# State-space entry of a two-block network: the norm's scale and shift applied by channel behind the turns

## The chip, the cores and the metric

One core of a Trainium2 chip. The metric is the device time of one execution in microseconds, the median of three runs where runs are given.

## What is computed

A first block of two layers (a gated delta rule with a feed-forward network; a state-space mixer, "S5", with a mixture of 8 experts) is followed by a second block with its own mixers and 32 experts. Sequence 256, width 1024, all in float32. The change is at the border of the first network and the S5 mixer, which the reference writes as

```
x = layer_norm(ALPHA * x + swiglu(x, w1, w3, w2), ln_g[0, 1], ln_b[0, 1])
u = x @ s5_w_in                      # 1024 x 1024
... per group of 16 channels a complex diagonal recurrence, read out, gelu, GLU ...
x = layer_norm(ALPHA * x + h, ln_g[1, 0], ln_b[1, 0])
```

with `layer_norm(x, g, b) = (x - mean) * rsqrt(var + eps) * g + b`. The normed x is needed twice: turned (channels on partitions) as the operand of `x @ s5_w_in`, and in rows (tokens on partitions) as the residual that the next sum uses.

## The kernel before

The 256 rows lie in `xres` as two halves of 128 tokens on partitions, 1024 channels along the free axis. A quarter is 512 channels of a half. Products keep about float32 accuracy by splitting every operand into a rounded high part and a low remainder: high by high, high by low and low by high are summed in PSUM. ACT copies the high part (`dn_high`), DVE subtracts to get the low one (`dn_low`), in place in the weight ring. The ring holds three units of 128x4096, loaded by SP, each when the unit three before it has been used. The high parts have three buffers taken in turn, so `dn_high` of piece p waits until PE has used piece p - 3.

The order of each engine's work is written out by hand; semaphores link the engines.

**Norm before S5.** `ffn_vector` (L1295) sums and takes statistics half by half (L1319, L325 to L342); ACT takes the root (`norm_root`, L379). DVE's `norm_half` (L348) then computes the rows in two passes a half with the scale row `lnp[:, 0]` (L355) and the shift row `lnp[:, 1]` (L359); both are loaded by SP late in the network (L3390), because their place serves as a weight buffer until then. PE turns each 128x128 block by a transpose (`turn_half`, L386, transposes at L392) into banks 0 to 3. ACT evacuates a quarter at a time into `xT_r`, rounded (`turn_evacuate`, L421), and DVE subtracts that from PSUM to make the low part `s5_x_low` (L1326).

**PE around it** (program order from L3462 on): last products of the network, `own_step` and the router sums (which need nothing of x), `awake(16, 4)`, turn of half 0, `awake(6, 4)`, turn of half 1. `awake(n, b)` issues n products of the identity whose result nobody reads. Each shows as two records.

**`s5_tensor`** (L1532). The input product has eight pieces of 128 output channels. `projected(c)` makes one: 24 matmuls, into bank 0 or 1 in turn; `dn_columns_high` does the 16 that need only the high part of x, `dn_columns_rest` the other eight. ACT evacuates each to `uT`. `driven(q)` multiplies channels into states, 64 small matmuls, into banks 2 to 5, for q = 0 to 7. The order is: piece 0, piece 1, drive 0, piece 2, piece 3, drive 1, piece 4, ... , and `driven(0)` first waits for `ln_scaled` at 6 (L1543), because bank 5 holds the router sums until DVE has read them (`router_sums_vector`, L1496: L1500 and L1501; the second raises `ln_scaled` to 6).

**`s5_vector`** (L1733) begins with `dn_low` of piece 3, `router_sums_vector`, and then rounds: turn the drive by cosines and sines (L1745, L1746), `dn_low` of two more pieces, sum (L1752, L1753), scan (L1761), turn back (L1770, L1771), sum (L1777, L1778).

**`s5_scalar`** (L1646) and **`s5_gpsimd`** (L1720): ACT makes `dn_high` of piece c + 3, waits for piece c, evacuates it; at pieces 3, 4 and 5 it also copies blocks out of PSUM (`own_blocks`) into `k_own`, two of which lie in `lnp`. GpSimd clears `lnp` for this once the rows are normed (L1725), makes eight diagonals (L1728) and adds them (L1731).

Of the kernel before, what the change touches and what calls it, by code (L numbers as in the profile page):

```python
# [16 lines left out]
F32 = mybir.dt.float32  # L17
# [7 lines left out]
P = 128  # L25
# [9 lines left out]
STEP = 4  # L35
# [37 lines left out]
def program(nc, I, out, upto="all"):  # L73
    ctx = ExitStack()
    with ctx:
# [19 lines left out]
        neg_own, ident_own = negm[:, 0:CHUNK], negm[:, CHUNK:]  # L95
        small = sb("small", [P, 56])
        smalli = sb("smalli", [P, 4], I32)
# [20 lines left out]

        cs = Carver(small, 0, 56)
        stats = cs(HALVES, 2, 6)  # L120
        mv = cs(HALVES, 2)
        rstd = cs(HALVES, 1)
        rtmp = cs(HALVES, 1)
# [14 lines left out]
        s5_d = cs(DC)  # L138
        ln_cols = cs(2, DC)
        w_ln = cs(2, DC, EXPERTS)  # L140
        w_ln_sum = cs(2, 4, EXPERTS)
# [1099 lines left out]
        def ffn_scalar(act):  # L1241
# [40 lines left out]
            for p in range(3):  # L1282
                dn_high(act, D_S5IN + p)
            norm_scalar(act, 1)
            turn_evacuate(act, 1, None, xT_r)

# [8 lines left out]
        def ffn_vector(v):  # L1295
# [19 lines left out]
            for h in range(HALVES):  # L1315
                v.wait_ge(sem("ffn_used"), FF_LAST + h + 1)
                for j in range(2):
                    xs = xres[:, h, 512 * j:512 * j + 512]
                    ins = v.scalar_tensor_tensor(xs, xs, ALPHA, bank[2 * h + j][:, :], ALU.mult, ALU.add)  # L1319
                    norm_stats(v, 1, xres, h, j, ins)  # L1320
            norm_vector(v, 1, xres, xres)
            for h in range(HALVES):
                for q in range(2):
                    o = (slice(None), slice(4 * q, 4 * q + 4), slice(h * P, (h + 1) * P))
                    v.wait_ge(sem("xT_ready"), 4 + 2 * h + q + 1)
                    v.tensor_tensor(s5_x_low[o], bank3(2 * h + q), xT_r[o].bitcast(F32), ALU.subtract)\  # L1326
                     .then_inc(sem("xl_ready"), 1)
            dn_low(v, D_S5IN + 2)

        def half_product(v, o, a_1, b_1, a_2, b_2, tmp, op):  # L1330
# [150 lines left out]
        def router_sums_gpsimd(g):  # L1481

            g.wait_ge(sem("router_loaded"), 80)
            for m in range(2):
                g.tensor_tensor(w_ln[:, m, :, :], w_r1, bc(ln_cols[:, m, :], 2, EXPERTS), ALU.mult).then_inc(sem("ln_scaled"), 1)
            for i, n in enumerate((4, 2, 1)):
                g.wait_ge(sem("ln_scaled"), 2 + i)
                parts = (w_ln, w_ln_sum)[i > 0]
                g.tensor_tensor(w_ln_sum[:, :, 0:n, :], parts[:, :, 0:n, :], parts[:, :, n:2 * n, :], ALU.add).then_inc(sem("ln_scaled"), 1)
# [42 lines left out]
        def s5_tensor(pe):  # L1532
# [44 lines left out]

            pe.wait_ge(sem("xl_ready"), 4 + 1)
            dn_columns_high(pe, D_S5IN, bank[0][:, 0:SEQ], xT_r)
            pe.wait_ge(sem("xl_ready"), 8)  # L1580
            dn_columns_rest(pe, D_S5IN, bank[0][:, 0:SEQ], s5_x_low)
            for q in range(3):
                projected(2 * q + 1)
                driven(q)
                projected(2 * q + 2)
# [60 lines left out]
        def s5_scalar(act):  # L1646
# [16 lines left out]
            for c in range(DC):  # L1663
                if c in (1, 2):
                    decay_row(c - 1)
                if c == 3:
                    act.wait_ge(sem("k0_ps"), 1)
                    act.wait_ge(sem("s5_pool"), 4)
                if c >= 3 and c - 3 < STEP - 1:
                    own_blocks(c - 3)  # L1670
                if c + 3 < DC:
                    dn_high(act, D_S5IN + c + 3)
                act.wait_ge(sem("dense_used"), D_S5IN + c + 1)
                act.activation(uT[:, c, :], bank[c % 2][:, 0:SEQ], ACT.Copy).then_inc(sem("s5_u_done"), 1)
# [45 lines left out]
        def s5_gpsimd(g):  # L1720
# [3 lines left out]
            g.memset(k_own[0], 0.0).then_inc(sem("s5_pool"), 1)  # L1724
            g.wait_ge(sem("rows_normed"), rows_at(1) + 4)  # L1725
            g.memset(lnp[:, :, :], 0.0).then_inc(sem("s5_pool"), 1)
# [6 lines left out]
        def s5_vector(v):  # L1733
# [45 lines left out]

            dn_low(v, D_S5IN + 3)  # L1780
            router_sums_vector(v)
            for q in range(DC + 2):
                if q < DC:
                    turned_in(q)
                for c in (2 * q + 4, 2 * q + 5):
                    if c < DC:
                        dn_low(v, D_S5IN + c)
                if q >= 2:
                    out_summed(q - 2)
                if 1 <= q <= DC:  # L1790
                    summed(q - 1)
                if q >= 4:
                    hid_split(v, q - 4)
                if q == DC:
                    dn_low(v, D_GLU)
                if 1 <= q <= DC:
                    scanned(q - 1)
                    turned_out(q - 1)
# [1511 lines left out]
        def _(sp):  # L3310
# [48 lines left out]
            load_norm(sp, 0)  # L3359
            for name, dst in (("w_r1", w_r1), ("b_r1", b_r1), ("w_r2", w_r2), ("b_r2", b_r2), ("ln_cols", ln_cols)):  # L3360
                sp.dma_start(dst, I[name]).then_inc(sem("router_loaded"), 16)
# [246 lines left out]
def layouts(inp):  # L3608
# [24 lines left out]
    A["consts"], A["early"] = constants()  # L3633
    A["g_cols"] = np.stack([chunkcols(inp[n][0]) for n in ("g_mix_2", "g_ffn_2", "g_ple_2")], axis=1)
    A["ln_cols"] = np.stack([chunkcols(inp[n][1, 0]) for n in ("ln_g", "ln_b")], axis=1)
    A["conv2_w"] = inp["w_conv_2"][0].reshape(CONV2_TAPS, CW // P, P).transpose(2, 1, 0)
# [73 lines left out]
```

## Time and profile before

| | |
|---|---|
| median of 3 runs | 1590.62 us (1589.98 to 1591.07) |
| the profiled execution | 1593.2 us, its span 1591.3 us |
| PE busy | 1508.8 us, 95% |
| PE weight loads | 1132.9 us, 71% |
| DVE busy | 1019.4 us, 64% |
| ACT busy | 696.2 us, 44% |
| GpSimd busy | 34.8 us, 2% |
| chain that ended last | PE 75%, DVE 13%, DMA 7%, ACT 2%, issue 2% |

Busy shares are means over stages with different limits. PE's share includes the filler. The chain follows the work that ended last back in time, at each step to what released it; the timeline lists one engine's instructions in order with the idle time ahead of each and what ended it. Line numbers are those of the kernel before. The granted clock is 1.00 at 2.4 GHz and 0.50 at 1.2 GHz.

### The profile page before, as it was taken

Reading aid. Unit: us, or ns where it says so; the run is one execution under the profiler, and the core shown is the slowest. Engines: PE = TensorE matmul, PEld = TensorE weight load, DVE = VectorE, ACT = ScalarE, POOL = GpSimd, SP = SyncE. Lnnn points to the kernel's source line nnn. Section 1 sums busy time; section 2 is a strip of 40 time slices with the busy share of each in tenths; the row PEclk is TensorE's granted clock in tenths of the full one; section 3 lists DMA queues with packets and bytes.
Section 4 is the critical chain, followed back from the end, with each engine's and each line's share of the span. In section 5 each row is a group of like instructions: output and inputs, shape, how many; then the busy total and the mean of one; then the engine's idle time right before and its main releaser. Section 6 shows DMA issues by size and latency. Waiting matters only on the chain.

```text
span 1591.3 us, 24618 instructions
## 1 busy us (share of the span) xinstructions
PE 1508.8 (95%) x10552; PEld 1132.9 (71%) x10552; DVE 1019.4 (64%) x1446; ACT 696.2 (44%) x915; POOL 34.8 (2%) x34
## 2 busy tenths in 40 slices
PE   7999898999998999999999998999999999999986
PEld 7988778888997888888888887986434434443435
DVE  5776778999869688889888987785121121212127
ACT  5673335454443467667677675353101101110114
POOL 0000100000020000000000001000000000000001
PEclk9999999999999989999999999999999999999998
DMA  8431044344631449889989897378999999999981
GB/s 342 159 148 56 2 157 182 133 159 159 242 117 58 183 175 363 332 329 351 352 336 336 325 367 302 126 314 361 426 427 428 428 428 428 428 427 427 428 366 40
DMA packets 37841, 443.45 MB, mean 279 GB/s; under 512 B 5600, under 2 KB 6112, under 8 KB 10464
## 3 DMA queue, kind: packets, MB, share of 16 engines
q1 hardware_dynamic: 36576, 438.35, 68.9%
q10 hardware_dynamic: 1152, 3.46, 0.6%
q8 instruction: 87, 1.43, 0.4%
q14 instruction: 26, 0.21, 0.0%
HBM read 440.75 MB, written 1.05 MB: 278 GB/s over the span
## 4 chain that ended last, share of the span: by engine, by line
PE 75%; DVE 13%; DMA 7%; ACT 2%; issue 2%; SPq 0%; PEldq 0%; PEld 0%; ACTq 0%; DVEq 0%
PE psum L232 73%; DMA sb_spare<-moe_up 3%; DVE sb_ring_r L1304 2%; DMA sb_ring<-moe_wide 1%; DMA sb_ring<-ffn_wide 1%; DVE sb_split L2027 1%; DVE sb_work L2738 1%; DMA sb_lnp<-ln_rows 1%; PE psum L2534 1%; PE psum L2082 1%; DMA sb_work<-b_im 0%; DVE sb_work L1334 0%; DVE sb_ring_r L509 0%; DVE sb_work L1333 0%; DVE sb_work L1332 0%
## 5 line engine op out<-in xcount | busy, mean ns | idle before, releaser
L2027 DVE TENSOR_TENSOR sb_split<-sb_ring,sb_split 128x2048 fp32r<-128x2048 f32 (+1 forms) x144 | 301.1, 2110 | 44.8 <-ACT sb_split L2021 43.8
L232 PE MATMUL psum<-sb_work 64*64 64x64 f32 (+11 forms) x3392 | 285.9, 335 | 19.0 <-DVE sb_work L2738 7.8
L2021 ACT ACTIVATE sb_split<-sb_ring 128x2048 fp32r<-128x2048 f32 (+1 forms) x144 | 253.2, 1773 | 89.2 <-PE psum L232 60.6
L232 PE MATMUL psum<-sb_split 128*128 128x512 f32 (+1 forms) x912 | 268.7, 384 | 0.2 <-DVE sb_split L2341 0.2
L232 PEld LDWEIGHTS psum<-sb_work 128*64 128x64 f32 (+4 forms) x3392 | 148.6, 143 | 140.7 <-issue 119.5
L232 PE MATMUL psum<-sb_split,sb_lnp_r 128*128 128x512 f32 (+1 forms) x768 | 230.4, 374 | 1.4 <-DVE sb_split L2310 1.4
L232 PEld LDWEIGHTS psum<-sb_split 128*128 128x128 f32 x912 | 169.9, 188 | 30.7 <-DVE sb_split L2341 0.7
L232 PEld LDWEIGHTS psum<-sb_split,sb_lnp_r 128*128 128x128 f32 x768 | 142.7, 188 | 21.8 <-DVE sb_split L2310 1.6
L232 PE MATMUL psum<-sb_xT_r,sb_ring_r 128*128 128x256 f32 x512 | 144.3, 283 | 0.0
L2736 DVE TENSOR_TENSOR sb_work<-sb_work,psum 128x512 f32<-128x512 f32 x16 | 11.0, 689 | 169.4 <-ACT sb_work L2648 169.4
L2648 ACT ACTIVATE sb_work<-psum 128x512 f32<-128x512 f32 x16 | 9.6, 597 | 238.7 <-PE psum L232 238.7
L232 PE MATMUL psum<-sb_ring,sb_work 128*64 128x512 f32 (+1 forms) x448 | 104.7, 599 | 7.2 <-DVE sb_work L2738 4.7
L2706 DVE SCALAR_TENSOR_TENSOR sb_out_even<-psum,sb_work,sb_out_even 128x512 fp32r<-128x512 f32 x32 | 22.6, 747 | 130.4 <-ACT sb_out_even L2634 130.4
L232 PEld LDWEIGHTS psum<-sb_xT_r,sb_ring_r 128*128 128x128 f32 x512 | 98.2, 192 | 0.2
L232 PEld LDWEIGHTS psum<-sb_ring,sb_work 128*64 128x64 f32 (+1 forms) x448 | 33.7, 140 | 71.2 <-issue 63.4
L232 PE MATMUL psum<-sb_s_in_high,sb_gw_r 128*128 128x256 f32 x384 | 72.1, 289 | 11.5 <-DVE sb_ring_r L509 11.5
L2634 ACT ACTIVATE sb_out_even<-psum,sb_work 128x512 fp32r<-128x512 f32 x32 | 20.3, 684 | 136.4 <-PE psum L232 136.4
L232 PEld LDWEIGHTS psum<-sb_s_in_high,sb_gw_r 128*128 128x128 f32 x384 | 61.5, 195 | 13.1 <-DVE sb_ring_r L509 11.5
L232 PE MATMUL psum<-sb_xT_r,sb_lnp_r 128*128 128x256 f32 x224 | 64.1, 286 | 2.8 <-DVE sb_ring_r L1304 2.7
L232 PE MATMUL psum<-sb_ffn_r,sb_lnp_r 128*128 128x256 f32 x224 | 63.4, 283 | 0.0
L1304 DVE TENSOR_TENSOR sb_ring_r<-sb_ring,sb_lnp_r 128x1024 fp32r<-128x1024 f32 x43 | 52.5, 1224 | 16.0 <-ACT sb_lnp_r L1247 15.4
L2713 DVE TENSOR_TENSOR sb_xres<-sb_xres,psum 128x512 f32<-128x512 f32 x64 | 39.7, 682 | 30.7 <-PE psum L232 30.7
(468 smaller groups left out, 2677.7 us busy)
## 6 DMA issues: line engine op xcount, KB each, us to landing
sb_ring<-moe_wide SPq DMA_DIRECT2D x48, 2048.0 KB, 8.8
sb_work<-moe_up SPq DMA_DIRECT2D x33, 2048.0 KB, 25.2
sb_ring<-w_dense SPq DMA_DIRECT2D x23, 2048.0 KB, 8.5
sb_ring<-moe_last SPq DMA_DIRECT2D x24, 1536.0 KB, 8.3
sb_ring<-moe_up SPq DMA_DIRECT2D x18, 2048.0 KB, 25.1
sb_work<-moe_down SPq DMA_DIRECT2D x17, 2048.0 KB, 24.4
sb_ring<-ffn_wide SPq DMA_DIRECT2D x12, 2048.0 KB, 7.8
sb_ring<-moe_down SPq DMA_DIRECT2D x9, 2048.0 KB, 25.5
```

The lines of the kernel that those rows point to most:

```text
L232: return nc.tensor.matmul(o, lhsT, rhs, start=start, stop=stop, **kw)
L1304: v.tensor_tensor(ff_piece(ring_r, s), ff_piece(ring, s), ff_buffer(s).bitcast(F32), ALU.subtract)\
L2021: act.activation(wh[half_home(e, i)][:, 0:half_size(i)], half_raw(e, i), ACT.Copy).then_inc(sem("m1_high"), 1)
L2027: v.tensor_tensor(wl[home][:, 0:half_size(i)], half_raw(e, i), wh[home][:, 0:half_size(i)].bitcast(F32), ALU.subtract).then_inc(sem("m1_sp ...
L2082: ins = pe.transpose(o[:, c * P:(c + 1) * P], e_hid[:, c * P:(c + 1) * P], ident)
L2534: ins = pe.transpose(bank[2][:, c * P:(c + 1) * P], e_hid[:, c * P:(c + 1) * P], ident)
L2634: act.activation(out_even[:, 0, 512 * i:512 * i + 512], bank[4 + i][:, :], ACT.Copy, scale=gate_slot[:, (g - 1) % 2:(g - 1) % 2 + 1]).then ...
L2648: act.activation(e_silu[0], bank[0][:, :], ACT.Silu).then_inc(step, 1)
L2706: v.scalar_tensor_tensor(out_even[:, 1, d], bank[4 + i][:, :], gate_slot[:, (g - 1) % 2:(g - 1) % 2 + 1], out_even[:, 0, d].bitcast(F32), ...
L2713: v.tensor_tensor(xs, xs, combine_bank(i), ALU.add).then_inc(step, 1)
L2736: v.tensor_tensor(e_hid, e_silu[0], bank[1][:, :], ALU.mult).then_inc(step, 1)
L2738: v.tensor_copy(e_hidT[:, :, :], bank3(2)).then_inc(step, 1)
```

## The change

Before the turns the rows are only centred and scaled to unit variance; scale g and shift b are applied behind the turns, where they are one number for each partition. ACT makes the first half's rows, DVE the second's. ACT's evacuation becomes four operations a quarter. DVE makes the unrounded value itself, four operations a quarter, into `s5_hid`, and subtracts. The rows get g and b later, in `rows_finished`, on DVE between S5's first operations. PE takes the high part of piece 1 ahead of the rest of piece 0. ACT's `own_blocks` move two pieces later. A small input `ln1_cols` is loaded by one DMA more. GpSimd clears `lnp` when the rows are finished.

```diff
-        small = sb("small", [P, 56])
+        small = sb("small", [P, 57])
...
+        ln1_cols = cs(2, DC)
...
@@ ffn_scalar @@
-            norm_scalar(act, 1)
-            turn_evacuate(act, 1, None, xT_r)
+            norm_root(act, 1, 0)
+            act.wait_ge(sem("rstd_ready"), 2 * 1 + 1)
+            act_link(act, act.activation(shift, mv[:, 0, 0:1], ACT.Copy, scale=rstd[:, 0, :]))
+            act_link(act, act.activation(shift, shift, ACT.Copy, scale=-1.0))
+            for q in range(2):
+                f = slice(512 * q, 512 * q + 512)
+                act.activation(xres[:, 0, f], xres[:, 0, f], ACT.Identity, scale=rstd[:, 0, :], bias=shift)\
+                   .then_inc(sem("rows_normed"), 1)
+            norm_root(act, 1, 1)
+            act.wait_ge(sem("router_loaded"), 96)
+            for h in range(HALVES):
+                for q in range(2):
+                    act.wait_ge(sem("turned"), 4 * TSTAGE[1] + 2 * h + q + 1)
+                    for c in range(4):
+                        k = 4 * q + c
+                        ins = act.activation(xT_r[:, k, h * P:(h + 1) * P], turn_bank(1, h, q)[:, c * P:(c + 1) * P], ACT.Identity,
+                                             scale=ln1_cols[:, 0, k:k + 1], bias=ln1_cols[:, 1, k:k + 1])
+                    ins.then_inc(sem("xT_ready"), 1)
...
@@ ffn_vector @@
-            norm_vector(v, 1, xres, xres)
+            v.wait_ge(sem("rstd_ready"), 2 * 1 + 2)
+            for q in range(2):
+                f = slice(512 * q, 512 * q + 512)
+                v.tensor_scalar(xres[:, 1, f], xres[:, 1, f], mv[:, 1, 0:1], rstd[:, 1, :], ALU.subtract, ALU.mult)\
+                 .then_inc(sem("rows_normed"), 1)
+            v.wait_ge(sem("router_loaded"), 96)
             for h in range(HALVES):
                 for q in range(2):
                     o = (slice(None), slice(4 * q, 4 * q + 4), slice(h * P, (h + 1) * P))
                     v.wait_ge(sem("xT_ready"), 4 + 2 * h + q + 1)
-                    v.tensor_tensor(s5_x_low[o], bank3(2 * h + q), xT_r[o].bitcast(F32), ALU.subtract)\
-                     .then_inc(sem("xl_ready"), 1)
+                    for c in range(4):
+                        k = 4 * q + c
+                        ins = v.tensor_scalar(s5_hid[:, k, h * P:(h + 1) * P], turn_bank(1, h, q)[:, c * P:(c + 1) * P],
+                                              ln1_cols[:, 0, k:k + 1], ln1_cols[:, 1, k:k + 1], ALU.mult, ALU.add)
+                    dve_link(v, ins)
+                    v.tensor_tensor(s5_x_low[o], s5_hid[o], xT_r[o].bitcast(F32), ALU.subtract).then_inc(sem("xl_ready"), 1)
             dn_low(v, D_S5IN + 2)
+
+        def rows_finished(v, h):
+
+            if h == 0:
+                v.wait_ge(sem("lnp_loaded"), 32 * 2)
+            dve_link(v, v.tensor_tensor(xres[:, h, :], xres[:, h, :], lnp[:, 0, :], ALU.mult))
+            v.tensor_tensor(xres[:, h, :], xres[:, h, :], lnp[:, 1, :], ALU.add).then_inc(sem("s5_drive"), 1)
...
@@ s5_tensor @@
-            pe.wait_ge(sem("xl_ready"), 4 + 1)
+            pe.wait_ge(sem("xl_ready"), 4 + 2)
             dn_columns_high(pe, D_S5IN, bank[0][:, 0:SEQ], xT_r)
             pe.wait_ge(sem("xl_ready"), 8)
-            dn_columns_rest(pe, D_S5IN, bank[0][:, 0:SEQ], s5_x_low)
+            dn_columns_high(pe, D_S5IN + 1, bank[1][:, 0:SEQ], xT_r)
+            for c in range(2):
+                dn_columns_rest(pe, D_S5IN + c, bank[c][:, 0:SEQ], s5_x_low)
             for q in range(3):
-                projected(2 * q + 1)
+                if q > 0:
+                    projected(2 * q + 1)
                 driven(q)
                 projected(2 * q + 2)
...
@@ s5_scalar @@
-                if c == 3:
+                if c == 5:
                     act.wait_ge(sem("k0_ps"), 1)
                     act.wait_ge(sem("s5_pool"), 4)
-                if c >= 3 and c - 3 < STEP - 1:
-                    own_blocks(c - 3)
+                if c >= 5 and c - 5 < STEP - 1:
+                    own_blocks(c - 5)
...
@@ s5_gpsimd @@
-            g.wait_ge(sem("rows_normed"), rows_at(1) + 4)
+            g.wait_ge(sem("s5_drive"), 6)
             g.memset(lnp[:, :, :], 0.0).then_inc(sem("s5_pool"), 1)
...
@@ s5_vector @@
             dn_low(v, D_S5IN + 3)
+            rows_finished(v, 0)
             router_sums_vector(v)
             for q in range(DC + 2):
                 if q < DC:
                     turned_in(q)
                 for c in (2 * q + 4, 2 * q + 5):
                     if c < DC:
                         dn_low(v, D_S5IN + c)
+                if q == 0:
+                    rows_finished(v, 1)
...
@@ SP, start of the program @@
-            for name, dst in (("w_r1", w_r1), ("b_r1", b_r1), ("w_r2", w_r2), ("b_r2", b_r2), ("ln_cols", ln_cols)):
+            for name, dst in (("w_r1", w_r1), ("b_r1", b_r1), ("w_r2", w_r2), ("b_r2", b_r2), ("ln_cols", ln_cols),
+                              ("ln1_cols", ln1_cols)):
                 sp.dma_start(dst, I[name]).then_inc(sem("router_loaded"), 16)
```

## Rows read from the trace of the kernel before

**Rows 1.** Chain that ended last, 405 to 530 us: start, us, what.
```profile
429.54 10.02 DMA sb_lnp<-ln_rows
...
446.63 32.08 PE psum L232 x448
...
478.73 0.07 DVE sb_work L1745
```

**Rows 2.** Timeline of DVE: start, us, line, operation, count, idle before.
```profile
435.47 0.16 DVE L342 RECIPROCAL sb_small<-sb_small 128x1 f32<-128x1 f32 x1
...
438.73 0.16 DVE L342 RECIPROCAL sb_small<-sb_small 128x1 f32<-128x1 f32 x1
...
443.82 1.41 DVE L359 SCALAR_TENSOR_TENSOR sb_xres<-sb_xres,sb_small,sb_lnp 128x512 f32<-128x512 f32 x2
445.27 2.48 DVE L1326 TENSOR_TENSOR sb_hid_low<-psum,sb_xT_r 128x512 fp32r<-128x512 f32 x4
```

**Rows 3.** Timeline of PE, turns and first s5 matmuls.
```profile
437.90 3.82 PE L232 MATMUL psum<-sb_consts 128*128 128x128 f32 x32
441.85 1.32 PE L392 MATMUL psum<-sb_consts,sb_xres 128*128 128x128 f32 x8
...
444.62 1.32 PE L392 MATMUL psum<-sb_consts,sb_xres 128*128 128x128 f32 x8
...
448.65 1.12 PE L232 MATMUL psum<-sb_hid_low,sb_s_in_high 128*128 128x256 f32 x8
...
452.58 2.12 PE L232 MATMUL psum<-sb_work 32*128 32x64 f32 x64
```

**Rows 4.** Busy time by engine in one stretch (count), granted clock, DMA share, GB/s.
```profile
479.00:509.00 30.00, 25.40 (x759) 22.92 (x758) 29.34 (x56) 9.65 (x27) 0.00 (x0) 0.94 0.15 62
```

**Rows 5.** Timeline of ACT, evacuation of the turns and piece 3.
```profile
445.32 1.26 ACT L421 ACTIVATE sb_xT_r<-psum 128x512 fp32r<-128x512 f32 x2 [1.51 <-PE psum L392]
449.89 1.06 ACT L277 ACTIVATE sb_s_in_high<-sb_ring 128x1024 fp32r<-128x1024 f32 x1 [3.31 <-PE psum L232]
```

**Rows 6.** Instructions by line and shape: busy us, mean ns, idle before.
```profile
L841 ACT ACTIVATE sb_work<-psum,sb_front 128x128 f32<-128x128 f32 x32 | 8.7, 382 | 0.5 <-PE psum L653 0.4
...
L3122 DVE TENSOR_SCALAR sb_work<-sb_work 128x512 f32<-128x512 f32 x2 | 1.1, 537 | 0.0
```

**Rows 7.** Timeline of ACT, 128x128 from PSUM with a column as scale.
```profile
105.55 2.15 ACT L841 ACTIVATE sb_work<-psum,sb_front 128x128 f32<-128x128 f32 x8
```

**Rows 8.** Timeline of DVE, 128x128 copies from PSUM.
```profile
168.94 1.78 DVE L1060 COPY sb_work<-psum 128x128 f32<-128x128 f32 x8 [0.34 <-PE psum L232]
```

**Rows 9.** Timeline of DVE, piece 3, router sums, drive 1.
```profile
450.98 1.24 DVE L282 TENSOR_TENSOR sb_ring_r<-sb_ring,sb_s_in_high 128x1024 fp32r<-128x1024 f32 x1 [2.07 <-ACT sb_s_in_high L277]
452.14 0.15 DVE L1500 TENSOR_SCALAR sb_front<-psum 128x8 f32<-128x8 f32 x1
...
462.75 0.69 DVE L1745 TENSOR_TENSOR sb_work<-psum,sb_work 128x512 f32<-128x512 f32 x1 [2.57 <-PE psum L232]
```

**Rows 10.** Timeline of POOL.
```profile
445.29 1.81 POOL L1726 MEMSET sb_lnp<- 128x2048 f32 x1 [6.52 <-DVE sb_xres L359]
447.08 6.77 POOL L1728 TENSOR_SCALAR sb_spare<-sb_consts,sb_front 128x128 f32<-128x128 f32 x8
460.80 2.38 POOL L1731 TENSOR_TENSOR sb_work<-sb_work,sb_spare 128x1024 f32<-128x1024 f32 x1 [6.95 <-ACT sb_work L1661]
```

**Rows 11.** Waits of SP's queue, 0 to 60 us.
```profile
SPq L3314 <- PE psum L232: 27.1, 3, 15.3
```

**Rows 12.** Busy time and granted clock around two pauses of PE.
```profile
223.50:225.50 2.00, 0.01 (x1) 0.00 (x0) 1.97 (x4) 0.10 (x1) 0.00 (x0) 1.00 0.98 418
...
226.00:232.50 6.50, 5.74 (x25) 4.86 (x24) 1.88 (x4) 2.72 (x4) 1.25 (x5) 0.50 0.36 130
985.50:990.00 4.50, 0.00 (x0) 0.00 (x0) 4.03 (x11) 2.55 (x4) 4.50 (x3) 1.00 0.46 187
990.50:993.50 3.00, 3.00 (x14) 3.00 (x15) 2.96 (x3) 0.00 (x0) 1.23 (x1) 0.50 0.02 5
```

More of the change, by code:

```diff
@@ L116, in __call__ @@
                 return a
-        cs = Carver(small, 0, 56)
+        cs = Carver(small, 0, 57)
         stats = cs(HALVES, 2, 6)
         mv = cs(HALVES, 2)
+        shift = cs(1)
         rstd = cs(HALVES, 1)
@@ L1481, in router_sums_gpsimd @@
         def router_sums_gpsimd(g):
-            g.wait_ge(sem("router_loaded"), 80)
+            g.wait_ge(sem("router_loaded"), 96)
             for m in range(2):
@@ L3634, in layouts @@
     A["g_cols"] = np.stack([chunkcols(inp[n][0]) for n in ("g_mix_2", "g_ffn_2", "g_ple_2")], axis=1)
+    A["ln1_cols"] = np.stack([chunkcols(inp[n][0, 1]) for n in ("ln_g", "ln_b")], axis=1)
     A["ln_cols"] = np.stack([chunkcols(inp[n][1, 0]) for n in ("ln_g", "ln_b")], axis=1)
```

## The prediction

> **What bounds the kernel now.** I read the chain of waits between the first feed-forward network and the state-space stage first, then one engine at a time there, then rows elsewhere for prices. The chain names a transfer: the norm's scale and shift rows (`sb_lnp`), 10.02 us, ending at 439.56 [rows 1]. DVE then normalises four quarters, ending at 445.23, and splits the turned rows [rows 2]. But PE has its own clock here. After the router sums it issues a fixed filler burst of 32 records (`awake(16, 4)`) from 437.90 to 441.72, and only then turns the first half, at 441.85; the second half starts at 444.62 [rows 3]. So the entry has two floors close together, rows and filler, and taking away the rows' floor alone gains little.
>
> From 446.63 PE works without a pause for 32.08 us, and hands over to DVE at 478.73 [rows 1]. In 479 to 509 DVE is busy 29.34 of 30 us [rows 4]: DVE is the bound there, and its start is PE's fourth `driven` result. So whatever delays PE between 446.63 and 478.73 delays everything behind. I find nothing behind that gives it back: ring loads wait for PE's or DVE's own progress.
>
> **The entry, part by part.** (a) *Rows.* The first half's reciprocal is out at 435.63; ACT's root and two one-column steps, then two 128x512 passes at some 0.63 each (the size of its evacuations [rows 5]), end near 437.8. The second half's reciprocal is out at 438.89 [rows 2]; DVE's two passes at 0.537 [rows 6] end near 440.3. Both lie before the filler's end. The transfer no longer gates anything here, and the rows themselves cost nothing. If the filler were gone they would be the floor.
>
> (b) *Turns.* PE starts at about 441.75. Without a wait between the quarters, eight records take about 0.95 (3.82/32 each [rows 3]) and the next filler (12 records) 1.43, so the second half starts near 444.13, 0.5 earlier than before [rows 3].
>
> (c) *Evacuation by ACT.* Before: 0.63 a quarter. Now four 128x128 operations with a column as scale and another as bias. The nearest row is eight 128x128 operations out of PSUM with a column as scale, in 2.15 [rows 7], 0.25 from start to start: 1.0 a quarter. Bounds: 0.16, a quarter of a 128x512 [rows 5], and 0.38, one of the eight in full without overlap [rows 6]. First quarter from 441.75 + 0.70 = 442.45 (the distance from turn to ACT [rows 3, 5]); quarters end 443.45, 444.45, 445.83, 446.83. PE begins near 446.95 instead of 446.63: **+0.32**.
>
> Trace and page differ on (c): eight operations in 2.15 is 0.25 each [rows 7]. The Trainium skill, ScalarE: Activation LUTs, What ACT_TABLE_LOAD costs, says that an ACTIVATE takes 186 ns and 0.833 ns a column, each pointer operand adds some 93 ns, and neighbours overlap by some 93 ns. As an estimate from that page, two pointers make 0.39 an operation, and the shift below would be about 6.7 instead of 6.2. I take the trace's.
>
> (d) *Low part by DVE.* Before: four subtractions in 2.48 [rows 2]. Now each quarter has four 128x128 scale-and-shift operations out of PSUM, a link, and a subtraction. Eight 128x128 copies out of PSUM took 1.78 [rows 8], 0.22 each; with two column operands I take 0.25. Bounds: 0.22, and 0.54, the price of four times the columns with two column operands [rows 6]; the copies are nearer, in width and in PSUM. With the last one's latency and the link about 1.1, and 0.62 for the subtraction: 1.7 a quarter (bounds 1.5 and 2.8). From 443.5, four of them back to back end at 450.3. PE has finished the high part of piece 0 (16 matmuls, 2.02 [rows 3]) at 448.97 and waits for the last low quarter: **+1.38**. Before, the low parts were all there by 447.75 [rows 2] and PE did not wait.
>
> (e) *Order on PE.* The high part of piece 1 now stands ahead of the rest of piece 0: **+2.02** until piece 0 counts as used, at about 453.35; before it was 449.63 (eight matmuls from 448.65 at 0.12). The rest of piece 1 ends at 454.33. No work is added; it is only ordered otherwise.
>
> (f) *The stall.* This decides it. PE's `driven(0)` writes over the bank that holds the router sums, and waits for DVE to have read them (`ln_scaled` at 6). On DVE that reading stands behind `dn_low` of piece 3. That needs ACT's copy of piece 3, which needs the buffer of piece 0, free when piece 0 is used. Before, this chain just kept up: used 449.63, ACT 449.89 to 450.95, DVE 450.98, sums read from 452.14, PE on at 452.58 [rows 3, 5, 9]. The change puts `rows_finished(v, 0)` between: two linked 128x1024 operations. One such costs 1.16 from start to start [rows 9], so with the link 2.45: **+2.45**. New times: used 453.35, ACT 453.61 to 454.67, DVE 454.70, rows from 455.86, sums from 458.31, `driven(0)` at 458.75. PE stands from 454.33 to 458.75, 4.4 us with nothing issued; waiting behind it in its queue are all the other pieces and drives. Shift: 0.32 + 1.38 + 2.02 + 2.45 = **6.2**.
>
> (g) *The second half's rows* stand on DVE after piece 5, where it waited 2.57 before turning in drive 1, at 462.75 [rows 9]. They need 2.45: covered, by 0.1. If the cover were thinner they would cost at most 2.45.
>
> (h) *The rest.* GpSimd clears `lnp` only after those rows, near 469, and then needs 1.81 + 6.77 + 2.38 [rows 10] = 11.0, until 480; PE reads the result behind its fourth drive, at 478.73 + 6.2 = 484.9. Covered by 5. ACT's `own_blocks`, two pieces later, fall into its waits for later pieces. The one DMA more sits on SP's queue before the first ring reloads; SP stood 27.1 us waiting for PE in that stretch [rows 11], so its issue is hidden. One more column in `small` moves addresses; I cost that at nothing.
>
> (i) *PE's clock.* After 4.5 idle us from 985.5 the granted clock was 1.00 up to the end, then 0.50 over the next 3.0 busy us; after 2.0 idle us from 223.5 it was 0.50 for 6.5 us [rows 12]. That is 1.2 GHz instead of 2.4. Standing for 4.4 us should bring the same: PE works at half rate for some 3.3 us (the 3.0 and its edges), and loses half of that: **+1.6** (bounds 0 and 3.3, half of 6.5). The Trainium skill, TensorE: Matmul & The Clock Gate, Part 1: The HAM clock gate, says that idleness throttles the array and work releases it; by that rule, the trace agrees, the change pays for the stall twice.
>
> Sum against the profiled execution: 1593.2 + 6.2 + 1.6 = 1601.0 (its span 1591.3 becomes 1599.1). The median of the runs is 1590.62, 2.6 lower, so 1598.4. About 0.2% (3.2 us) is what can be told from no change.
>
> **The rivals.** *Stall, no clock loss* (13%): as above, but the half-rate stretch falls mostly into the stall: 1590.6 + 6.2 = 1596.8. For: the stall is long enough for the clock to fall and rise early. Against: in both examples the half rate lay over busy time [rows 12].
>
> *Hidden anyway* (11%): one part of (f) isn't there. DVE's read of the sums comes in time or the later stretch holds slack, and only the entry counts: 0.3 + 1.4 = 1.7, or less with cheap operations: 1592. Against: PE has no pause in 32.08 us [rows 1], so no slack is seen in which 4.4 could vanish; DVE at 98% behind it [rows 4] has none either.
>
> *The norm was the floor* (5%), faster. Place: from the second reciprocal to the first s5 matmul. If the modelled PE ends mislead and the filler is out earlier than 438, the turns follow the rows: ACT is done near 443 and PE starts 3.5 us earlier. Price: 1590.6 - 3.5 = 1587.1, if in addition DVE's quarters stay near 0.62 and the reading of the sums keeps pace. For: the chain view blames the transfer [rows 1]. Against: 3.82 us of filler is fixed and ends 2.8 us after the last reciprocal. It decides only when the filler ends before 438.
>
> *Dearer operations* (10%): ACT at 0.38, DVE half-way to its bound at 2.1 a quarter: the last low quarter ends at 452.4 instead of 450.3, a shift of 8.3; with the clock low for twice as long, +3.3: 1602.2.
>
> **How the numbers follow.** Forecast as worked out: 61%, 1598.4. With the dearer case and no clock loss 84% is slower by well over 0.2%; the hidden case has most of 11% within 0.2%; 5% faster. The range takes in the lower bounds of (c) and (d) without the clock, 1590.6 + 5.0 = 1595.6, some of the hidden case below it, and the dear one above: 1594 to 1602.5. The far bound of (d) lies outside.
>
> **What would show it.** Right: DVE's line for `rows_finished` between piece 3 and the sums; PE idle of some 4.4 us ahead of `driven(0)`, released by DVE's read of the sums; a clock of 0.50 behind it; drive 4 at DVE near 486.5 instead of 478.73; an idle of about 1.4 ahead of piece 1. (c) is wrong if ACT's sixteen take much other than 4 us. The whole is wrong if `driven(0)` starts before 455, or the time from 479 to the end shrinks by what came ahead of it.

## The result

The changed kernel takes 1603.54 us (median of 6 runs, 1601.83 to 1608.32) against 1590.70 for the kernel before (6 runs): 12.8 us slower by the medians, ratio 1.0085, interval 1.007 to 1.010. Forecast were 7.8. Its profiled execution took 1603.02, span 1600.9.

First the wait list of PE from 440 to 480 us in the changed kernel: engine, line and what it waited for, us in total, times, longest.

```profile
PE psum L234 <- DVE sb_front L1535: 4.2, 1, 4.2
PE psum L234 <- ACT sb_xT_r L1301: 3.3, 1, 3.3
PE psum L234 <- DVE sb_hid_low L1354: 1.2, 1, 1.2
```

The pause for the router sums (L1535) is there, at the size forecast. The one for DVE's last low part (L1354) is there too, 1.2 for the 1.4 forecast. The third, 3.3 us for ACT's evacuation ahead of the first product, was not forecast. In the kernel before PE waited 0.7 for ACT between its last turn and its first product, and then for nothing up to drive 4 [rows 1]. The same list for the kernel before has one line:

```profile
PE psum L232 <- ACT sb_xT_r L421: 0.7, 1, 0.7
```

The timelines of PE, ACT and DVE in the changed kernel show each step:

```profile
436.95 2.85 PE L234 MATMUL psum<-sb_work 128*32 128x96 f32 x128
...
439.97 3.82 PE L234 MATMUL psum<-sb_consts 128*128 128x128 f32 x32
443.62 1.04 PE L394 MATMUL psum<-sb_consts,sb_xres 128*128 128x128 f32 x8
444.50 1.50 PE L234 MATMUL psum<-sb_consts 128*128 128x128 f32 x12
445.84 1.04 PE L394 MATMUL psum<-sb_consts,sb_xres 128*128 128x128 f32 x8
450.14 0.36 PE L234 MATMUL psum<-sb_xT_r,sb_s_in_high 128*128 128x256 f32 x1 [3.27 <-ACT sb_xT_r L1301]
...
464.18 2.94 PE L234 MATMUL psum<-sb_work 32*128 32x64 f32 x64 [4.17 <-DVE sb_front L1535]
```

```profile
438.52 1.52 ACT L1292 ACTIVATE sb_xres<-sb_xres,sb_small 128x512 f32<-128x512 f32 x2
...
444.32 5.70 ACT L1301 ACTIVATE sb_xT_r<-psum,sb_front 128x128 fp32r<-128x128 f32 x16 [3.13 <-PE psum L394]
459.17 1.06 ACT L279 ACTIVATE sb_s_in_high<-sb_ring 128x1024 fp32r<-128x1024 f32 x1 [9.15 <-PE psum L234]
```

```profile
441.22 1.00 DVE L1342 TENSOR_SCALAR sb_xres<-sb_xres,sb_small 128x512 f32<-128x512 f32 x2 [0.27 <-ACT sb_small L383]
445.93 1.37 DVE L1351 TENSOR_SCALAR sb_work<-psum,sb_front 128x128 f32<-128x128 f32 x4 [3.71 <-ACT sb_xT_r L1301]
...
453.36 0.69 DVE L1354 TENSOR_TENSOR sb_hid_low<-sb_work,sb_xT_r 128x512 fp32r<-128x512 f32 x1
...
460.26 1.23 DVE L284 TENSOR_TENSOR sb_ring_r<-sb_ring,sb_s_in_high 128x1024 fp32r<-128x1024 f32 x1 [5.07 <-ACT sb_s_in_high L279]
461.40 1.22 DVE L1361 TENSOR_TENSOR sb_xres<-sb_xres,sb_lnp 128x1024 f32<-128x1024 f32 x1
462.65 1.22 DVE L1362 TENSOR_TENSOR sb_xres<-sb_xres,sb_lnp 128x1024 f32<-128x1024 f32 x1
463.80 0.16 DVE L1534 TENSOR_SCALAR sb_front<-psum 128x8 f32<-128x8 f32 x1
...
475.88 1.23 DVE L1362 TENSOR_TENSOR sb_xres<-sb_xres,sb_lnp 128x1024 f32<-128x1024 f32 x1
477.27 0.69 DVE L1782 TENSOR_TENSOR sb_work<-psum,sb_work 128x512 f32<-128x512 f32 x1 [0.17 <-PE psum L234]
...
487.53 1.85 DVE L1814 TENSOR_TENSOR sb_work<-sb_work 128x256 f32<-128x256 f32 x1
...
493.26 0.69 DVE L1782 TENSOR_TENSOR sb_work<-psum,sb_work 128x512 f32<-128x512 f32 x1 [0.29 <-PE psum L234]
```

The rows are normed by 442.2, filler ends at 443.8: the filler holds the turns, as forecast. Counted from the network's end the turns start 0.3 and 0.85 us earlier than before. ACT's sixteen take 5.70, not 4. From 445.93 to 454.05 DVE makes four quarters without a pause, some 2.0 each. Piece 3 is copied at 459.17, and L1361, L1362 then stand between its low part and the sums.

The same kernel by stretch: us, PE busy (count), weight loads, DVE, ACT, POOL, granted clock, DMA share, GB/s.

```profile
446.90:450.10 3.20, 0.00 (x0) 0.00 (x0) 3.13 (x9) 3.12 (x9) 0.00 (x0) 1.00 0.00 0
...
451.80:458.00 6.20, 4.97 (x24) 4.67 (x23) 3.35 (x7) 0.00 (x0) 0.00 (x0) 0.50 0.00 0
...
460.00:464.00 4.00, 0.01 (x1) 0.00 (x0) 3.71 (x5) 2.92 (x8) 0.00 (x0) 1.00 0.00 0
465.50:471.40 5.90, 5.90 (x52) 5.78 (x49) 2.42 (x3) 0.00 (x0) 0.00 (x0) 0.50 0.01 3
```

Behind both pauses the clock is 0.50 (1.2 GHz), over nearly busy stretches: twice what I had allowed for.

**The measure used below.** S is the time from PE's first `own_step` product, right behind the network, to DVE's turning of the fourth drive. The fourth (q = 3) is called drive 4, as in the prediction; drives 0 and 1 are q = 0 and q = 1. In the kernel before these are

```profile
434.88 2.85 PE L232 MATMUL psum<-sb_work 128*32 128x96 f32 x128
```

and 478.73 [rows 1]: S = 43.85. In the changed kernel S = 493.26 - 436.95 = 56.31, 12.46 more. What lies behind S took 1112.6 and 1107.6 in these two profiles, and 1106 to 1118 in all fourteen. So in this one profile of the changed kernel the rest was 5.0 shorter; in a second one (e10 below) it took 1112.1, so S is not paid back behind it. On the chips of the experiments the kernel before alone ran from 1583.1 to 1601.7, so S decides and the ratio of whole times checks. All columns but the last two are us from the first `own_step` product: "first product" is PE's first of piece 0, "p3" ACT's copy of piece 3, "sums" DVE's read of the router sums, "drive 0" PE's start of it. "low" is the us of S at half clock.

| kernel | first product | p3 | sums | drive 0 | S | low | ratio to before, interval |
|---|---|---|---|---|---|---|---|
| before | 11.75 | 15.01 | 17.26 | 17.70 | 43.85 | 0 | |
| changed | 13.19 | 22.22 | 26.85 | 27.23 | 56.31 | 13.7 | 1.0085 (1.007-1.010) |
| e1 sums first | 13.19 | 21.67 | 23.90 | 24.28 | 53.37 | 10.2 | 1.0061 (1.0038-1.0085) |
| e2 filled | 13.18 | 20.39 | 25.02 | 25.55 | 51.69 | 0 | 1.0055 (1.0037-1.0074) |
| e3 plain evacuation | 10.67 | 15.84 | 20.47 | 20.85 | 49.53 | 6.8 | 1.0037 (1.0015-1.0059) |
| e4 old order | 13.19 | 18.49 | 23.12 | 23.50 | 52.65 | 10.2 | 1.0050 (1.0033-1.0067) |
| e5 before, late sums | 11.61 | 14.87 | 19.61 | 19.99 | 46.15 | 0 | 1.0019 (0.9998-1.0039) |
| e6 before, no filler | 13.86 | 19.46 | 21.69 | 22.14 | 48.30 | 13.7 | 1.0003 (0.9983-1.0023) |
| e7 repaired | 9.96 | 15.26 | 14.92 | 16.64 | 42.80 | 0 | 0.9998 (0.9981-1.0015) |
| e8 scale only | 12.33 | 19.17 | 23.80 | 24.18 | 54.22 | 13.7 | one run |
| e9 | 11.22 | 18.11 | 14.77 | 18.62 | 44.78 | 3.4 | 0.9993 (0.9972-1.0015) |
| e10 changed again | 13.19 | 22.13 | 26.76 | 27.14 | 56.23 | 13.7 | 1.0084 (1.0052-1.0115) |
| e11 | 9.22 | 15.38 | 14.78 | 15.89 | 42.05 | 0 | 1.0001 (0.9985-1.0016) |
| e12 sums first, filled | 13.19 | 20.41 | 22.64 | 23.33 | 49.47 | 0 | 1.0085 (1.0055-1.0114) |

From drive 0 to drive 4 it is 26.14 to 26.16 in every kernel whose clock was full there, and 28.7 to 30.0 where it was not.

### The profile page after: what moved, and what is told of

It reads as the page before. It is cut to its first block, busy times and chain, and to the rows that moved or that the text cites. A ratio compares the mean times of both kernels' runs of the same rounds, so it can differ in the third digit from the quotient of the medians.

```text
span 1600.9 us, 24649 instructions
## 1 busy us (share of the span) xinstructions
PE 1509.2 (94%) x10552; PEld 1135.1 (71%) x10552; DVE 1026.0 (64%) x1460; ACT 701.2 (44%) x931; POOL 35.6 (2%) x34
## 3 DMA queue, kind: packets, MB, share of 16 engines
q8 instruction: 87, 1.43, 0.4%
HBM read 440.75 MB, written 1.05 MB: 276 GB/s over the span
## 4 chain that ended last, share of the span: by engine, by line
PE 76%; DVE 13%; DMA 5%; ACT 2%; issue 2%; SPq 0%; PEldq 0%; PEld 0%; ACTq 0%; DVEq 0%
PE psum L234 74%; DMA sb_spare<-moe_up 3%; DVE sb_ring_r L1322 2%; DMA sb_ring<-moe_wide 1%; DVE sb_split L2067 1%; DVE sb_work L2778 1%; DMA sb_ring<-ffn_wide 1%; PE psum L2574 1%; PE psum L2122 1%; DMA sb_work<-b_im 1%; DVE sb_work L1368 0%; DVE sb_ring_r L511 0%; DVE sb_work L1367 0%; DVE sb_work L1366 0%; DVE sb_work L1798 0%
```

## The experiments

The theory after the result: four delays in a row on the way to drive 0 (dearer evacuation, dearer low parts, PE's order, rows ahead of the sums), and the clock lost behind the pauses. The main rival: the added work alone, with the clock beside it.

**e1: the sums read first.**

```diff
             dn_low(v, D_S5IN + 3)
-            rows_finished(v, 0)
             router_sums_vector(v)
+            rows_finished(v, 0)
```

> The changed kernel with one thing swapped on DVE: the router sums are read before rows_finished(0), not behind it. Theory (the time is lost in a pause of PE that the two row operations lengthen, and in the clock behind it): driven(0) starts 2.45 us earlier against the end of the network, PE's pause before it falls from 4.2 to about 1.7 us, and the rows then fit into DVE's wait for the first drive; 2.45 us less, up to 4.5 less if the shorter pause spares the half clock: 1599 to 1601 against 1603.5. Rival (the rows cost where they stand on DVE, wherever that is): no change, 1603.5, with the wait moved to drive 0. Rival (the sums' read is the whole cause): back to the kernel before, 1590.7.

From p3 to the sums it is 2.23 instead of 4.63: the rows cost 2.40 there, and nothing where they now stand. S falls by 2.94. As a whole time e1 (median 1603.24) cannot be told from the changed kernel; it is S that refutes the rival of no change. The clock fell all the same behind the remaining pause of 1.6:

```profile
PE psum L234 <- ACT sb_xT_r L1301: 3.3, 1, 3.3
PE psum L234 <- DVE sb_hid_low L1354: 1.8, 1, 1.8
PE psum L234 <- DVE sb_front L1535: 1.6, 1, 1.6
```

The rival that the read of the sums is the whole cause falls: S is still 9.5 over the kernel before.

**e2: the pauses filled.** Nothing changes on ACT and DVE.

```diff
                 turn_half(pe, 1, xres, 1)
+                awake(13, 4)
                 pe.wait_ge(sem("xT_ready"), 4 * (TSTAGE[1] + 1))
...
             dn_columns_high(pe, D_S5IN, bank[0][:, 0:SEQ], xT_r)
+            awake(5, 4)
             pe.wait_ge(sem("xl_ready"), 8)
...
                 if q == 0:
+                    awake(16, 4)
                     pe.wait_ge(sem("ln_scaled"), 6)
```

> The changed kernel with filler products of the identity in PE's three pauses: 13 ahead of the first s5 product, 5 ahead of the wait for the last low part, 16 ahead of driven(0). Nothing on ACT or DVE changes. Theory (the pauses also cost the clock: some 1.9 us on pieces 0 and 1 and 2.9 us from drive 0 to drive 3): the granted clock stays at 1.00 from 440 to 480, and the time falls by about 4.8 us, to 1598.7. Rival (the half clock lies beside waits that are there anyway, the total half-rate time of both kernels being the same 60 us): no change within 1 us, 1603.5.

By stretch, all of S:

```profile
437.75:489.40 51.65, 50.04 (x708) 48.31 (x707) 37.25 (x63) 22.77 (x54) 12.81 (x11) 1.00 0.31 117
```

The clock is 1.00 throughout and S falls by 4.62, against 4.8 expected: the clock's part is shown. Without it the rest is clean. Against the kernel before the first product comes 1.43 later; from there to p3 it is 7.21 instead of 3.26, 3.95 more; from p3 to the sums 2.38 more; together 7.84 with the edge. The whole time fell by only 1.3 on medians (2.2 against e10, the changed kernel on the same chip); its ratio gives 8.8 over the kernel before (5.9 to 11.8), which holds 7.84. So the rival is refuted in the stage, and the whole time could not have told it.

**e3: the evacuation of the kernel before.** Leaves out scale and shift on the turned operand.

```diff
@@ ACT @@
-                    for c in range(4):
...
-                    ins.then_inc(sem("xT_ready"), 1)
+                    o = (slice(None), slice(4 * q, 4 * q + 4), slice(h * P, (h + 1) * P))
+                    act.activation(xT_r[o], bank3(2 * h + q), ACT.Copy).then_inc(sem("xT_ready"), 1)
@@ DVE @@
-                    for c in range(4):
...
-                    dve_link(v, ins)
-                    v.tensor_tensor(s5_x_low[o], s5_hid[o], xT_r[o].bitcast(F32), ALU.subtract).then_inc(sem("xl_ready"), 1)
+                    v.tensor_tensor(s5_x_low[o], bank3(2 * h + q), xT_r[o].bitcast(F32), ALU.subtract).then_inc(sem("xl_ready"), 1)
```

> The changed kernel with the evacuation of the kernel before: one ACT copy of 128x512 a quarter and one DVE subtraction; it leaves out the scale and shift on the turned operand. Theory (the dearer evacuation costs its own time and, by PE's pause of 3.3 us ahead of the first product, the clock): PE's first s5 product comes 2.3 us earlier, no wait for the low part, clock 1.00 until the pause before driven(0), piece 0 used some 6 us earlier: 1597.5. Rival (only the operations' own time counts, clock apart): 2.3 + 1.7 = 4.0 us less, 1599.5. Rival (DVE's rows are the main part, the evacuation hides): 1602 or more.

First product 2.52 earlier, p3 6.38 earlier, S 6.78 less, one low stretch less. Evacuation and low parts with what they do to the clock are the largest part. The first product is even 1.1 ahead of the kernel before: this is what the early rows are worth. It is still slower by 5.7 in S: 1.91 from first product to p3 (PE's order), 2.38 for the rows, 2.5 from drive 0 to drive 4 for the clock, less the 1.1.

**e4: PE's old order.**

```diff
-            dn_columns_high(pe, D_S5IN + 1, bank[1][:, 0:SEQ], xT_r)
-            for c in range(2):
-                dn_columns_rest(pe, D_S5IN + c, bank[c][:, 0:SEQ], s5_x_low)
+            dn_columns_rest(pe, D_S5IN, bank[0][:, 0:SEQ], s5_x_low)
             for q in range(3):
-                if q > 0:
-                    projected(2 * q + 1)
+                projected(2 * q + 1)
```

> The changed kernel with PE's order of before: all of piece 0, then all of piece 1, then drive 0. Theory (the wait chain ACT copy of piece 3, DVE low part, rows, sums starts when piece 0 is used): piece 0 is used 2.0 us earlier at full clock, 3.5 at half clock, and driven(0) with it; piece 1 lies in the pause. Time 2 to 3.5 us less: 1600 to 1601.5. The pause shrinks from 4.2 to about 2 us. Rival (the order is neutral, since the work is the same): 1603.5.

p3 and drive 0 come 3.73 earlier, S falls by 3.66, the pause to 2.2. The order is not neutral: it delays the piece that the chain of ACT, DVE and the sums waits for. That is 2.02 at full clock; the clock was low here for the rest.

**e5: two operations ahead of the sums in the kernel before.**

```diff
             dn_low(v, D_S5IN + 3)
+            rows = xres[:, 0, :]
+            for _ in range(2):
+                dve_link(v, v.tensor_tensor(rows, rows, rows, ALU.max))
             router_sums_vector(v)
```

> The kernel before with two linked DVE operations of 128x1024 (the maximum of the first half's rows with themselves, which leaves them as they are) between the low part of piece 3 and the read of the router sums; nothing else. Theory: driven(0) starts 2.45 us later, PE pauses about 2.5 us ahead of it, and the time grows by 2.5 us, or by 4.1 where the pause also brings a stretch at half clock: 1593.2 to 1594.8. Rival (slack behind takes it up): 1590.7.

```profile
PE psum L232 <- DVE sb_front L1501: 2.4, 1, 2.4
```

The pause is there, the clock did not fall, S grows by 2.30: nothing up to drive 4 takes it up. The ratio, 3.0 us with an interval from -0.3 to 6.2, agrees, but would not show it alone.

**e6: the kernel before without filler at the entry.**

```diff
                 router_sums_tensor(pe)
-                awake(16, 4)
                 turn_half(pe, 1, xres, 0)
-                awake(6, 4)
                 turn_half(pe, 1, xres, 1)
```

> The kernel before without the two filler bursts at the entry (16 and 6 products of the identity): PE pauses some 3.8 and 1.4 us there. Theory (pauses cost the clock on the products that follow): ACT and DVE as before, the granted clock falls to 0.50 on pieces 0 and 1 or drive 0 for at least 3 us, and the time grows by 1.6 to 3.3 us: 1592.3 to 1594. Rival (the turns were held by the filler, so without it they come earlier): no growth, or 0.2 us less, 1590.5.

S grows by 4.45, more than expected, but not all is the clock. The timeline of DVE shows the transfer of scale and shift landing later in this execution:

```profile
443.06 1.42 DVE L355 SCALAR_TENSOR_TENSOR sb_xres<-sb_xres,sb_small,sb_lnp 128x512 f32<-128x512 f32 x2 [2.17 <-DMA sb_lnp<-ln_rows]
```

443.06 - 436.88 = 6.18 after the network's end, against 4.71 in the kernel before: 1.47 of S. The other 3.0 are half clock: 0.65 on the turns, 2.33 from the first product to drive 0. So the filler is worth 3 us of S, and the old way does hang on that transfer, which landed 1.5 us apart in these two profiles. The whole time shows no difference, 0.5 us with an interval from -2.7 to 3.7.

**e8: one column operand.** Leaves out the shift on the turned operand.

```diff
@@ ACT @@
-                        ins = act.activation(xT_r[:, k, h * P:(h + 1) * P], turn_bank(1, h, q)[:, c * P:(c + 1) * P], ACT.Identity,
-                                             scale=ln1_cols[:, 0, k:k + 1], bias=ln1_cols[:, 1, k:k + 1])
+                        ins = act.activation(xT_r[:, k, h * P:(h + 1) * P], turn_bank(1, h, q)[:, c * P:(c + 1) * P], ACT.Copy,
+                                             scale=ln1_cols[:, 0, k:k + 1])
@@ DVE @@
-                                              ln1_cols[:, 0, k:k + 1], ln1_cols[:, 1, k:k + 1], ALU.mult, ALU.add)
+                                              ln1_cols[:, 0, k:k + 1], None, ALU.mult)
```

> The changed kernel with the shift left out on the turned operand (the sixteen operations of ACT and of DVE have one column operand, the scale, where they had two). It prices the second column operand. Theory (each column operand has a price of its own, and the row I forecast from had one): ACT's sixteen take about 4.1 us instead of 5.70, 0.25 each, and DVE's four about 1.15 instead of 1.36; PE's first product comes 1.1 us earlier and drive 4 some 1.5 to 3 us earlier, for the clock. Rival (the width or the rounded output makes 0.36 an operation): 5.7 and 1.36 as in the changed kernel.

The timelines of ACT and DVE:

```profile
444.90 4.34 ACT L1301 ACTIVATE sb_xT_r<-psum,sb_front 128x128 fp32r<-128x128 f32 x16 [3.13 <-PE psum L394]
```

```profile
446.15 1.13 DVE L1351 TENSOR_SCALAR sb_work<-psum,sb_front 128x128 f32<-128x128 f32 x4 [3.34 <-ACT sb_xT_r L1301]
```

5.70 - 4.34 = 1.36 over sixteen: the second column operand costs ACT 0.085 us an operation. On DVE four fall from 1.37 to 1.13, 0.06 each. With one operand ACT's price is 0.26 from start to start, that of [rows 7]. The rival, width or rounding, is refuted. ACT's function changed with the operand, from Identity to Copy, and DVE's addition went with its operand; what is priced is each operand together with that. The first product came 0.86 earlier (1.1 expected) and drive 0 3.05 earlier, but S fell by only 2.09: the low stretch at drive 0 was 10.2 us here instead of 6.8.

**e10: the changed kernel again.**

> The changed kernel itself, unaltered, beside the others on this chip. Theory (what lies behind drive 4 varies with the clock from run to run, the stage does not): drive 4 at 56 us from the network's end, within 1.5, and the ratio within 1.006 to 1.010. Rival (the 12.5 us of the first profile were a chance of the clock's phase): drive 4 below 53.

S = 56.23 and the ratio 1.0084: the stage repeats to 0.1 us, its two low stretches too.

**e7, e9, e11: versions meant to beat both.** e7 reads the sums ahead of the low part of piece 3, takes both high parts ahead of the wait, and starts the turns at once, since the rows are ready.

```diff
+            router_sums_vector(v)
             dn_low(v, D_S5IN + 3)
             rows_finished(v, 0)
-            router_sums_vector(v)
...
             dn_columns_high(pe, D_S5IN, bank[0][:, 0:SEQ], xT_r)
-            pe.wait_ge(sem("xl_ready"), 8)
             dn_columns_high(pe, D_S5IN + 1, bank[1][:, 0:SEQ], xT_r)
+            pe.wait_ge(sem("xl_ready"), 8)
...
-                awake(16, 4)
                 turn_half(pe, 1, xres, 0)
-                awake(6, 4)
+                awake(5, 4)
                 turn_half(pe, 1, xres, 1)
+                awake(14, 4)
```

> The changed kernel repaired: the router sums are read at once, ahead of the low part of piece 3; PE takes the high parts of pieces 0 and 1 before it waits for the last low part; no filler ahead of the first turn, 5 products between the turns, 14 behind. The rows of the first half are ready by the end of the router sums, so the turns start some 3.5 us earlier than in the changed kernel. Theory: ACT's sixteen operations (0.36 each) then end near 445 on the time axis of the kernel before, PE's first product starts about 1.5 us earlier than in the kernel before, the last low part comes near 449, driven(0) near 451.5, clock at 1.00: 1589 to 1590.7, equal to the kernel before or 1 us better. Rival (DVE's eight microseconds of low parts bound the entry wherever they begin): driven(0) near 453 and 1592. Rival (rows_finished(0) costs wherever it stands): 1593.

S = 42.80, 1.05 under the kernel before: the four delays no longer show in S, with the same work on ACT and DVE. The first product came 1.8 earlier than before.

e9 is e7 with 12 products in the place of its 14, and two edits more. It has ACT only round the last quarter, from DVE's value, and evacuates piece 0 ahead of `dn_high` of piece 3.

```diff
@@ DVE; value(h, q) is the four operations of a quarter, low(h, q) its subtraction @@
+            value(0, 0)
+            value(1, 1).then_inc(sem("x_value"), 1)
+            v.wait_ge(sem("x_value"), 1)
+            low(0, 0)
+            for h, q in ((0, 1), (1, 0)):
+                dve_link(v, value(h, q))
+                low(h, q)
+            low(1, 1)
@@ ACT, in the place of the last quarter's four @@
+            act.wait_ge(sem("x_value"), 1)
+            act.activation(xT_r[:, 4:8, P:2 * P], s5_hid[:, 4:8, P:2 * P], ACT.Copy).then_inc(sem("xT_ready"), 1)
@@ ACT, pieces @@
-                if c + 3 < DC:
+                if 0 < c and c + 3 < DC:
                     dn_high(act, D_S5IN + c + 3)
...
                 act.activation(uT[:, c, :], bank[c % 2][:, 0:SEQ], ACT.Copy).then_inc(sem("s5_u_done"), 1)
+                if c == 0:
+                    dn_high(act, D_S5IN + 3)
```

> The repaired kernel (e7) with two more edits: DVE makes the value of the last quarter early and ACT only rounds it, one 128x512 copy in the place of four operations; and ACT evacuates piece 0 before it copies piece 3. Theory (ACT's sixteen bound the entry, and PE then waits 0.5 us for piece 0's evacuation): first product 0.75 us earlier than in e7, at 9.2 us from the network's end, drive 4 at 41.5 instead of 42.8 (43.85 in the kernel before). The whole some 2.3 us under the kernel before, 0.15%, about at what can be told. Rival (DVE's eight microseconds are the floor): drive 4 at 42.3 to 42.8, no gain over e7.

It missed: the first product came at 11.22. PE's wait ahead of piece 0 asks for two low parts, and DVE's early value had pushed the second one behind. The pause, again, brought a low stretch.

```profile
PE psum L234 <- issue: 2.4, 1, 2.4
```

e11 mends that. Against e9:

```diff
-            pe.wait_ge(sem("xl_ready"), 4 + 2)
+            pe.wait_ge(sem("xl_ready"), 4 + 1)
             dn_columns_high(pe, D_S5IN, bank[0][:, 0:SEQ], xT_r)
+            pe.wait_ge(sem("xl_ready"), 4 + 2)
             dn_columns_high(pe, D_S5IN + 1, bank[1][:, 0:SEQ], xT_r)
```

> e9 with PE's wait ahead of piece 0 lowered to the first low part (which frees bank 0), and the wait for the second put ahead of piece 1's high part. In e9 DVE's early value of the last quarter had pushed the second low part behind, and PE stood 2.4 us for it. Theory: first product 9.2 us from the network's end (11.75 in the kernel before, 9.96 in e7), no half clock on pieces 0 and 1, drive 4 at 41.4 (43.85 before, 42.8 in e7); the whole about 2.4 us under the kernel before, ratio 0.9985. Rival (DVE's last low part, 13.7 us from the end, bounds it anyway): first product 9.2, but piece 0 used no earlier than in e7, drive 4 at 42.3.

```profile
PE psum L234 <- ACT sb_xT_r L1307: 0.5, 1, 0.5
PE psum L234 <- DVE sb_hid_low L1363: 0.4, 1, 0.4
```

First product at 9.22 as expected, S = 42.05, 1.80 under the kernel before. But 41.4 was expected, and the rival is nearer: PE waits for DVE's last low part all the same, and the rest of piece 0 begins 13.78 us from the network's end, against 13.92 in e7. Most of the 0.75 won over e7 is ACT's evacuation of piece 0 ahead of its copy of piece 3: in e7 PE stood 0.55 for that ahead of drive 0, here not at all. As whole times e7, e9 and e11 cannot be told from the kernel before: all three intervals hold 1. That a gain of 1 to 2 us in the stage reaches the end is not shown.

**e12: e1 and e2 together,** the last filler cut to 6.

> The changed kernel with both edits of e1 and e2: sums read first, and fillers (13, 5 and 6) in the pauses. Theory: the terms add up once the clock is held: 7.84 (e2's shift of drive 4 against the kernel before) less 2.38 for the rows = 5.4, so drive 4 at 49.3 from the network's end and the granted clock at 1.00 through the stage. Rival (the rows then hold DVE at drive 0 and delay what follows): 50.5 or more.

S = 49.47: the terms add up. The whole time does not follow: 13.5 us over the kernel before (8.7 to 18) in four runs, where 5.6 was due. In its profile what lies behind S took 1117.7, the most of all fourteen. It has some 14 us at half clock from 54.7 on the scale of the table, 5 us behind drive 4; the chain shows PE just before without a releaser, and then at work:

```profile
487.94 1.20 issue
489.14 15.23 PE psum L234 x282
```

Part of the excess may be this clock behind the stage, but it is not shown: e10 has a stretch as long, from 65.5 on, and took 1112.1 behind S. Why the clock fell there, and whether it does in every run, stays open.

## Why the prediction was wrong

Direction, place and mechanism held; the size did not. The steps that failed are (c) and (d), the prices of ACT's and DVE's operations, and (i), the price of the clock. By the prediction's steps:

- (a), (b): right. Rows by 442.2 against a filler end of 443.8, turns 0.3 and 0.85 earlier than before when counted from the network's end (0.1 and 0.5 forecast).
- (c), wrong by 1.1: +0.32 forecast, +1.43 measured (e2). I took 0.25 an operation from a row with one column operand and let the second come free; it was 0.36. e8 shows the missing part to go with that operand. The row was one of another form. The Trainium skill, ScalarE: Activation LUTs, What ACT_TABLE_LOAD costs, says some 93 ns for each pointer operand; e8 agrees with 85, and the estimate of 0.39 that stood beside mine was nearer than mine.
- (d), wrong by 0.6: +1.38 forecast, 1.93 measured (3.95 from first product to p3 in e2, less 2.02 for the order). 2.01 a quarter instead of 1.7; the second column operand is 0.24 of it (e8).
- (c) and (d) do not act one by one: piece 0 waits for the last low part, and DVE makes its four quarters without a pause. Along that path the same 1.7 us come 0.4 from ACT's first quarter and 1.3 from DVE's four, so DVE's price is what held piece 0, and a shorter ACT alone mostly moves the wait, as e11 shows.
- (e): right. 2.02 forecast, 2.01 at full clock in e2 (sixteen matmuls from 454.89 to 456.90); e4 gives 3.66 with the low clock over it.
- (f): right, and the best part: 2.45 forecast, 2.40 in e1, 2.38 in e2, 2.30 in e5; the pause was 4.2 against 4.4.
- (g), (h): right up to drive 4. The second half's rows (474.63 to 477.11) end right ahead of drive 1 at 477.27. GpSimd's work is covered for PE, but now runs beside DVE's, and I had not asked what that costs DVE: the one operation L1814 took 1.85 us, 0.42 for the same one in the kernel before.

```profile
486.69 2.40 POOL L1768 TENSOR_TENSOR sb_work<-sb_work,sb_spare 128x1024 f32<-128x1024 f32 x1
```

It came out of DVE's wait ahead of drive 4 (2.0 us before, 0.3 here) and cost S nothing: in e2, which has it too, drive 0 to drive 4 is 26.14, against 26.15 in the kernel before.

- (i), wrong by 3: +1.6 forecast, 4.62 measured. I priced one pause and one low stretch of 3.3 us. There were two, 6.8 us each. The one behind the stall cost 2.94 (drive 0 to drive 4, 29.08 against 26.14 in e2) for the 1.6 forecast. The other cost 1.68 (drive 0 at 27.23 against 25.55); it lay behind the pause ahead of the first product, 3.3 instead of the 0.7 of before, which (c) had made longer and which I had not priced at all. My own row of the 6.5 us stretch [rows 12] was the better example.

6.2 + 1.6 became 7.84 + 4.62 = 12.46. The case "dearer operations" had this mechanism at 11.6, with 10%; I had set my range too close to the forecast, and an error in (c) feeds (i) as well, so the terms' bounds do not act one by one. "Stall, no clock loss" is refuted by e2, "hidden anyway" by S, and "the norm was the floor" by e7 in a telling way: with the filler gone the early rows do bring the first product 1.8 us forward, which pays only once the sums and the order are mended.

## What to carry to other kernels

Before an operation is put between two others on one engine, follow what is queued behind it up to the matmul engine: 2.4 us of harmless-looking work cost 2.4 us and a pause, while a few lines further on it was free. Take a price from a row with the same number of column operands, not only the same shape. And price every pause of TensorE at its own length plus a range for the half clock behind it, from nothing (e5) to the 2.9 us measured here; in a hand-ordered stage either move the work or put filler into the pause.

## What was not expected of the hardware

The half clock behind a pause does not follow from the pause's length alone. Two pauses of 3.3 us (with 1.2 close behind) and 4.2 us were each followed by some 6.8 us at 1.2 GHz in both profiles of the changed kernel, and a remaining pause of 1.6 us in e1 as well. Yet the same 3.3 us brought only 3.4 us in e1 and e4, and the 4.2 us brought 10.2 in e8. A pause of 2.4 us in e5 was followed by none, and one of 2.4 us in e9 by 3.4 us. The second column operand costs 0.085 us on ACT and 0.06 us on DVE in an operation of 128x128 out of PSUM, each with the change of function or operation that went with it.

In all eleven profiles in which GpSimd's 128x1024 addition runs while DVE works on the third drive, one DVE operation of 128x256 takes 1.85 us. In the kernel before, where GpSimd is done by then, it takes 0.42. Why that one and not its neighbours is not shown.
